# A ring of fourteen gathered pairs in place of ten, in the memory of the split buffers

## The chip, the core and the metric

The kernel runs on one core of a Trainium2 chip. The metric is the device time of one execution in microseconds (us). The engines of the core are named as in the profile: PE is TensorE (matmuls; PEld its weight loads), DVE is VectorE, ACT is ScalarE, POOL is GpSimd and SP is SyncE. All DMAs run on 16 DMA engines that the core has.

## What is computed

Two blocks of two layers each on 256 tokens of width 1024, in float32. The first block holds attention, a convolution and, twice, the `peer_ffn` with which this change deals: each token chooses experts by two small score tables per head, fetches one row of 1024 values from each of two tables for every chosen expert, takes the inner product of the first with its own input, and adds the second rows with the resulting weights.

```python
def peer_ffn(h, w_query, sub_keys, u_tab, v_tab):        # for a block of 128 tokens, 8 heads
    q = (hb @ w_query).reshape(128, PEER_HEADS, 2, half)
    s = jnp.einsum("thpd,hpnd->thpn", q, sub_keys)
    s_top, i_top = lax.top_k(s, PEER_TOPK)               # 16 of 128, in each half
    ...
    best, pos = lax.top_k(cand, PEER_TOPK)               # 16 of the 256 sums
    expert = jnp.take_along_axis(cand_idx, pos, axis=-1)
    gate = jax.nn.softmax(best, axis=-1)
    u = jnp.take(u_tab, expert, axis=0)
    act = jax.nn.gelu(jnp.einsum("thkd,td->thk", u, hb), approximate=False)
    return jnp.einsum("thk,thkd->td", gate * act, jnp.take(v_tab, expert, axis=0))
```

The second block is, per layer, a gated feed-forward (`ffn`), a mixer (`mix`) and another gated feed-forward.

## The kernel before

The phases run in one order on all engines (line 115): ada, attn 0, peer 0, conv 0, peer 1, then ffn, mix, ffn for each of the two layers of the second block. Every engine has its own instruction stream, in order; semaphores tie them together.

**A peer phase.** There are `PICKS` = 256 picks in a layer: 8 heads x 2 token blocks x 16 choices. A pick is one gathered pair for 128 tokens: for each partition (token) one row of 2048 float32, the u row and the v row side by side, 8 KB a partition and 1.05 MB in all. The steps of a pick k:

- GpSimd (lines 805 to 819) issues the indirect gather into slot k % `PAIR_RING` of the ring. Every 16 picks it first waits for the choice that names the experts (`expert_ready`); from pick `PAIR_RING` on it waits until TensorE has used the pair that lay in the slot (`v_used`, line 812). In layer 0 slot 7 is preceded by a wait for TensorE's reads of the attention output that lies there (`LATE_SLOT`).
- VectorE waits for the landing and takes the dot of u with the input (line 2350), and one pick later multiplies by the gate (`weigh`, line 2357).
- ScalarE applies gelu (line 1124) and writes a 128 x 128 diagonal of the weights (line 1131) into one of `DIAGS` = 8 places; from the ninth on it waits for `v_used` too.
- TensorE multiplies diagonal by v into PSUM (line 1727; one call per half of the row, in all four matmul records a pick) and raises `v_used`.
- The last `LAST` = 4 picks of a layer are added up by VectorE (`add_row`, lines 2359 to 2366), which raises `v_used` by 4 at line 2398.

In between, at the picks of `CHOOSE_AT` (line 64), VectorE makes the next choice of 16 experts (`choose`), and at those of `QUERY_AT` TensorE computes the next head's query and scores (lines 1420, 1717), which ScalarE copies out of PSUM (line 997). The phase opens with the first head for token block 0, then the late outputs and norms of token block 1, then the first head for block 1.

GpSimd's other work around the phase: after peer 0 it waits for all of its picks (line 781) and loads 14 weight rows (line 783). SP streams weight tiles of 512 KB into 4 slots (line 727) throughout.

**The memory.** The ring `uv` of ten pairs is the last part of the `arena`, a buffer that every phase carves in its own way. Outside the arena stand `w_hi`, `w_lo`, `a_hi` and `a_lo` (lines 392 to 395), 8 KB a partition each. They hold the two-part splits of weights and activations for the ffn and mix blocks; nothing before the first ffn touches them. The first to write there is ScalarE's `open_split` (called at line 1199, converting at line 896), which in its stream stands right behind the last peer phase's copies of y (line 1158); VectorE subtracts at line 2086.

Line 2968 reserves 4096 bytes a partition for the descriptors of GpSimd's DMAs.

Of the kernel before, what the change touches and what calls it, by code (L numbers as in the profile page):

```python
# [10 lines left out]
F32 = mybir.dt.float32  # L11
# [3 lines left out]
ALU = mybir.AluOpType  # L15
# [4 lines left out]
P = 128  # L20
D = 1024
KC = D // P
# [17 lines left out]
LAYERS = 2  # L40
# [6 lines left out]
HALF = D // 2  # L47
# [7 lines left out]
PICKS = H * TB * TOPK  # L55
SPAN, LAST = 1, 4
# [10 lines left out]
LATE_SLOT = 7  # L67
TAPPED = [6, 7]
EARLY_TAPS = 16
PAIR_RING = 10  # L70
TAP_ROWS = 8
DIAGS = 8
ADA_PARTS = [(0, 0, 4), (0, 4, 12), (1, 0, 4), (1, 4, 12)]
# [298 lines left out]
def bass_two_blocks(nc, stream, mod_rows_in, c_rows, x_cols, ctx_cols, cols_in, const_in, tab_attn, tab_mix, rpb_windows, keys_in, gain_rows,  # L372
# [5 lines left out]
    with ExitStack() as ctx:  # L378
        def sb(name, shape, dt=F32):
            return ctx.enter_context(nc.sbuf_tensor(name, shape, dt))  # L380
# [8 lines left out]
        sq = sb("sq", [P, KC * T])  # L389
        a_in = sq[:, :].rearrange("p (c t) -> p c t", c=KC)  # L390

        w_hi = sb("w_hi", [P, 2, D], F32R)
        w_lo = sb("w_lo", [P, 2, D], F32R)
        a_hi = sb("a_hi", [P, KC, T], F32R)
# [34 lines left out]
        def carve(sizes):  # L429
            at, got = 0, {}  # L430
            for name, n in sizes:
# [32 lines left out]
                  for name in ("ctx", "pt") for e in range(2)]  # L464
# [2 lines left out]
                   ("s2", TB * 2 * NKEY), ("tv", 64), ("ti", 64), ("tf", 64), ("cand", TB * 256), ("cand2", TB * 256),  # L467
                   ("bv", 32), ("bp", 32), ("ab", 128), ("eq", TB * 256), ("res", 64), ("inv", 1), ("idx", PICKS),
                   ("gate", PICKS), ("raw", PICKS), ("act", PICKS), ("w", PICKS), ("diag", DIAGS * P),
                   ("uv", PAIR_RING * 2 * D)])  # L470
        sub_keys = R["keys"].rearrange("p (m n) -> p m n", m=2 * H)
        h_rows = R["hb"].rearrange("p (b n) -> p b n", b=TB)
        pq = R["q"].rearrange("p (r e t) -> p r e t", r=LEAD, e=2)
# [13 lines left out]
        expert = R["idx"].bitcast(U32)  # L487
        gate, act_raw, act_out, act_w = R["gate"], R["raw"], R["act"], R["w"]
        diag = R["diag"].rearrange("p (r n) -> p r n", r=DIAGS)
        pair_ring = R["uv"].rearrange("p (r n) -> p r n", r=PAIR_RING)  # L490
        u_part, v_part = pair_ring[:, :, 0:D], pair_ring[:, :, D:2 * D]
        y_rows = sq[:, :].rearrange("p (b n) -> p b n", b=2 * TB)

        act_ring = sq[:, 0:2 * T].rearrange("p (b t) -> p b t", b=2)
# [276 lines left out]
        def _(pool):  # L771
# [34 lines left out]
            def peer(l):  # L806
                base = PICKS * l
                for k in range(PICKS):
                    if k % TOPK == 0:
                        pool.wait_ge(expert_ready, CHOICES * l + k // TOPK + 1)  # L810
                    if base + k >= PAIR_RING:
                        pool.wait_ge(v_used, base + k - PAIR_RING + 1)
                    if l == 0 and k == LATE_SLOT:
                        last = PL["peer", l]["t_late"][KC - 1]
                        pool.wait_ge(tile_done[last.unit], last.first)
                    pool.indirect_dma_start(  # L816
                        out=pair_ring[:, k % PAIR_RING, :], out_offset=None, in_=experts[l],
                        in_offset=bass.IndirectOffsetOnAxis(ap=expert[:, k:k + 1], axis=0)) \
                        .then_inc(pair_landed[k % PAIR_RING], 16)

# [10 lines left out]
        def _(act):  # L831
# [362 lines left out]
            def ffn(f):  # L1194
                pl = PL["ffn", f]
                l, j = f // 2, f % 2
                s = BLOCKS.index(("ffn", f))
                if s == 0:
                    open_split(f)
                if PART_BASE["ffn", f]:  # L1200
                    act.wait_ge(part_used, PART_BASE["ffn", f])
# [197 lines left out]
        def _(pe):  # L1399
# [301 lines left out]
            def peer(l):  # L1701
# [19 lines left out]
                def values(n):  # L1721
                    b = n % PER_HEAD // PER_CHOICE
                    for k in range(SPAN * n, SPAN * (n + 1)):
                        pe.wait_ge(diag_ready, TURNED * l + k + 1)
                        pe.wait_ge(pair_landed[k % PAIR_RING], landed(l, k))
                        for half in range(2):
                            ins = pe.matmul(ps[:, 2 * b + half, :], diag[:, k % DIAGS, :],  # L1727
                                            v_part[:, k % PAIR_RING, HALF * half:HALF * (half + 1)],
                                            start=(k == TOPK * b), stop=(k == (TURNED if b == TB - 1 else PICKS - TOPK * (TB - 1 - b)) - 1),
                                            skip_group_check=True)  # L1730
                        ins.then_inc(v_used, 1)
# [276 lines left out]
        def _(dve):  # L2008
# [256 lines left out]
            def peer(l):  # L2265
# [79 lines left out]
                def dots(n, first, end):  # L2345
                    b = n % PER_HEAD // PER_CHOICE
                    for k in range(first, end):
                        u = u_part[:, k % PAIR_RING, :]
                        dve.wait_ge(pair_landed[k % PAIR_RING], landed(l, k))
                        dve.scalar_tensor_tensor(out=u, in0=u, scalar=1.0, in1=h_rows[:, b, :], op0=ALU.mult,  # L2350
                                                 op1=ALU.mult, accum_out=act_raw[:, k:k + 1]).then_inc(dot_done, 1)
# [5 lines left out]
                    dve.tensor_tensor(act_w[:, part], act_out[:, part], gate[:, part], ALU.mult).then_inc(weighed, 1)  # L2357

                def add_row(k):
                    row, w = v_part[:, k % PAIR_RING, :], act_w[:, k:k + 1]  # L2360
                    dve.wait_ge(weighed, WEIGHED * l + GROUPS + k - TURNED + 1)
                    if k == TURNED:
                        link(dve.tensor_scalar(row, row, w, None, ALU.mult))
                    else:
                        link(dve.scalar_tensor_tensor(out=row, in0=row, scalar=w, in1=v_part[:, (k - 1) % PAIR_RING, :],
                                                      op0=ALU.mult, op1=ALU.add))

                choose(0)
# [23 lines left out]
                dve.wait_ge(v_used, base + TURNED)  # L2392
                for half in range(2):
                    dve.tensor_tensor(y_rows[:, 2 + half, :], ps[:, 2 + half, :],
                                      v_part[:, (PICKS - 1) % PAIR_RING, HALF * half:HALF * (half + 1)], ALU.add) \
                        .then_inc(y_copied, 1)
                dve.wait_ge(y_copied, 2 * TB * (l + 1))
                dve.sem_inc(v_used, LAST)
# [579 lines left out]
```

## Time and profile before

| | us |
|---|---|
| median of 3 runs | 3013.23 |
| lowest, highest | 3011.79, 3018.31 |
| profiled execution | 3023.53 |
| its span | 3021.7 |
| mean granted TensorE clock in it | 0.947 |
| PE busy | 2624.4 (87%) |
| DVE busy | 1952.7 (65%) |
| ACT busy | 1112.2 (37%) |
| POOL busy | 627.7 (21%) |

The profile is of one execution. Its slices cut the span in 40 equal parts of some 75.5 us; a digit is a tenth of the slice. Windows are stretches in us from the start of the span; their DMA share is the mean busy share of the 16 DMA engines. In the list of groups the idle time behind the last bar is that of the engine just before these instructions, with what ended it. Peer 0 runs from about 338 to 1035 us of the span, peer 1 from about 1200 to 1900 us.

### The profile page before, as it was taken

The page shows a single profiled execution, that of the slowest core. Times are in us where ns is not written, and L with a number is a line of the kernel's source. Part 1 is how long each engine was busy: PE and PEld are TensorE (multiplying, and loading weights), DVE is VectorE, ACT ScalarE, POOL GpSimd, SP SyncE. Part 2 cuts the span into 40 slices and gives each one's busy share as a digit, 9 for nine tenths or more (in the row PEclk, how much of TensorE's full clock was granted, in tenths as well). Part 3 has the DMA queues.
Part 4 walks back from the last instruction along what each step waited for, and adds up shares of the span by engine and source line. Part 5 has one row for each costly group of instructions (what it writes and reads, how often), then busy time and mean ns, then how long its engine had stood idle before and what let it go on. Part 6 is the DMA issues. An engine that isn't in the chain of part 4 may idle for free. (4 is left out here: it accounts for less than half of the span.)

```text
span 3021.7 us, 36197 instructions
## 1 busy us (share of the span) xinstructions
PE 2624.4 (87%) x11546; PEld 1729.6 (57%) x11546; DVE 1952.7 (65%) x4771; ACT 1112.2 (37%) x2639; POOL 627.7 (21%) x600
## 2 busy tenths in 40 slices
PE   7989888888877697788888877799989999999998
PEld 3534744333332386543333332798848989985798
DVE  1866467776676586667766775666746666675565
ACT  3245232222222322322222221445535454464544
POOL 0400134444444200244344443000000000000000
PEclk9989999999989898899999899899989999999999
DMA  9930889999999834899999999455415545552454
GB/s 307 387 150 1 321 327 420 417 413 417 409 415 417 353 110 141 334 409 417 416 419 416 408 413 420 170 187 175 159 53 177 185 160 188 184 161 83 147 183 151
DMA packets 152951, 832.42 MB, mean 275 GB/s; under 512 B 17008, under 2 KB 17136, under 8 KB 86384
## 3 DMA queue, kind: packets, MB, share of 16 engines
q0 software_dynamic: 85392, 579.38, 47.0%
q1 hardware_dynamic: 65664, 238.65, 23.8%
q10 hardware_dynamic: 1760, 12.70, 1.3%
q8 instruction: 71, 1.16, 0.2%
q14 instruction: 64, 0.52, 0.0%
HBM read 829.61 MB, written 1.05 MB: 275 GB/s over the span
## 5 line engine op out<-in xcount | busy, mean ns | idle before, releaser
L1727 PE MATMUL ps<-arena 128*128 128x512 f32 x2016 | 964.1, 626 | 253.7 <-ACT arena L1131 253.4
L1727 PEld LDWEIGHTS ps<-arena 128*128 128x128 f32 x2016 | 382.4, 198 | 825.4 <-ACT arena L1131 431.4
L2350 DVE SCALAR_TENSOR_TENSOR arena<-arena 128x1024 f32<-128x1024 f32 x512 | 626.1, 1224 | 329.5 <-DMA arena<-experts,arena 329.3
L816 POOL DMA_INDIRECT arena<-experts,arena x512 | 571.3, 1116 | 1104.1 <-PE ps L1727 745.9
L2086 DVE TENSOR_TENSOR w_lo<-weights,w_hi 128x512 fp32r<-128x512 f32 x528 | 364.3, 691 | 281.9 <-ACT w_hi L896 280.0
L1131 ACT ACTIVATE arena<-con,arena 128x128 f32<-128x128 f32 x504 | 203.0, 403 | 750.0 <-DVE arena L2357 750.0
L896 ACT ACTIVATE w_hi<-weights 128x512 fp32r<-128x512 f32 x528 | 332.9, 632 | 376.8 <-PE ps L1666 280.1
L1664 PE MATMUL ps<-a_hi,w_hi 128*128 128x256 f32 x1408 | 400.4, 284 | 5.8 <-DVEq L2105 2.7
L1665 PE MATMUL ps<-a_lo,w_hi 128*128 128x256 f32 x1408 | 399.6, 284 | 0.0
L1666 PE MATMUL ps<-a_hi,w_lo 128*128 128x256 f32 x1408 | 399.5, 284 | 0.0
L1664 PEld LDWEIGHTS ps<-a_hi,w_hi 128*128 128x128 f32 x1408 | 271.1, 193 | 10.6 <-DVEq L2105 3.1
L1665 PEld LDWEIGHTS ps<-a_lo,w_hi 128*128 128x128 f32 x1408 | 271.2, 193 | 3.1
L1666 PEld LDWEIGHTS ps<-a_hi,w_lo 128*128 128x128 f32 x1408 | 271.1, 193 | 0.0
L1420 PE MATMUL ps<-sq,weights 128*128 128x256 f32 (+1 forms) x1088 | 210.1, 356 | 22.0 <-ACT sq L890 16.4
L1420 PEld LDWEIGHTS ps<-sq,weights 128*128 128x128 f32 x1088 | 187.1, 202 | 48.6 <-issue 24.4
L997 ACT ACTIVATE arena<-ps 128x256 f32<-128x256 f32 (+5 forms) x182 | 83.3, 462 | 236.3 <-PE ps L1420 136.1
L1675 PE MATMUL ps<-w_hi,v_hi 128*128 128x512 f32 x352 | 138.5, 394 | 4.7 <-DVE v_lo L2506 4.7
L1675 PE MATMUL ps<-w_hi,v_lo 128*128 128x512 f32 x352 | 138.1, 392 | 0.0
L1675 PE MATMUL ps<-w_lo,v_hi 128*128 128x512 f32 x352 | 137.0, 389 | 0.0
L2357 DVE TENSOR_TENSOR arena<-arena 128x1 f32<-128x1 f32 x512 | 79.9, 156 | 73.1 <-ACT arena L1124 73.0
L2060 DVE SCALAR_TENSOR_TENSOR arena<-arena,mod_rows 128x1024 f32<-128x1024 f32 x71 | 93.6, 1344 | 33.5 <-DMA arena<-mod_rows_in 32.3
L1420 PE MATMUL ps<-arena,weights 128*128 128x128 f32 (+3 forms) x480 | 104.9, 378 | 4.4 <-ACT arena L890 2.2
(274 smaller groups left out, 3090.4 us busy)
## 6 DMA issues: line engine op xcount, KB each, us to landing
weights<-stream SPq DMA_DIRECT2D x453, 512.0 KB
arena<-mod_rows_in POOLq DMA_DIRECT2D x71, 512.0 KB, 8.8
arena<-experts,arena POOLq DMA_INDIRECT x512
mod_rows<-mod_rows_in POOLq DMA_DIRECT2D x9, 512.0 KB, 8.7
arena<-gain_rows ACTq DMA_DIRECT2D x1, 3072.0 KB, 11.5
arena<-rpb_windows ACTq DMA_DIRECT2D x4, 512.0 KB, 17.5
arena<-keys_in ACTq DMA_DIRECT2D x2, 1024.0 KB, 7.6
arena<-tab_mix ACTq DMA_DIRECT2D x2, 768.0 KB, 4.1
```

Source lines behind the costliest of these rows:

```text
L816: pool.indirect_dma_start(out=pair_ring[:, k % PAIR_RING, :], out_offset=None, in_=experts[l], in_offset=bass.IndirectOffsetOnAxis(ap=expe ...
L896: act.activation(w_hi[:, o % 2, part], weights[:, t.unit, part], ACT.Copy).then_inc(hi_ready, 1)
L1131: act.activation(diag[:, k % DIAGS, :], const("ident"), ACT.Copy, scale=act_w[:, k:k + 1]).then_inc(diag_ready, 1)
L1420: ins = pe.matmul(dst, wt(t, k, a, b), rhs(k), start=(k == 0), stop=(k == KC - 1))
L1664: pe.matmul(dst, w_hi[:, o % 2, cut], a_hi[:, k, :], start=(k == 0), stop=False)
L1665: pe.matmul(dst, w_hi[:, o % 2, cut], a_lo[:, k, :], start=False, stop=False)
L1666: ins = pe.matmul(dst, w_lo[:, o % 2, cut], a_hi[:, k, :], start=False, stop=(k == KC - 1))
L1675: ins = pe.matmul(ps[:, 2 * tb + half, :], v[:, b, at], w[:, o % 2, cut], start=(start and n == 0), stop=False, skip_group_check=True)
L1727: ins = pe.matmul(ps[:, 2 * b + half, :], diag[:, k % DIAGS, :], v_part[:, k % PAIR_RING, HALF * half:HALF * (half + 1)], start=(k == TOPK ...
L2060: dve.scalar_tensor_tensor(out=tile, in0=tile, scalar=1.0, in1=c_row, op0=ALU.mult, op1=ALU.mult, accum_out=mod[:, l, m, 0:1]).then_inc(ro ...
L2086: dve.tensor_tensor(w_lo[:, o % 2, part], weights[:, t.unit, part], w_hi[:, o % 2, part].bitcast(F32), ALU.subtract) \
L2350: dve.scalar_tensor_tensor(out=u, in0=u, scalar=1.0, in1=h_rows[:, b, :], op0=ALU.mult, op1=ALU.mult, accum_out=act_raw[:, k:k + 1]).then_ ...
```

## The change

The ring gets fourteen slots. Slots 0 to 9 stay in the arena. Slots 10 to 13 lie in a tensor `held` of 32 KB a partition that is laid out at the place of `w_hi`, `w_lo`, `a_hi` and `a_lo`, which are then laid out over it: one pair a buffer. `pair_of`, `u_of` and `v_of` give a pick's slot in either place. There are fourteen landing semaphores in place of ten. ScalarE waits, ahead of the first split of the first ffn, until `v_used` is 2 x 256 - 4 = 508, which is when TensorE has used its last pair. The number of gathers, dots, diagonals and matmuls is as before.

```diff
-PAIR_RING = 10
+ARENA_PAIRS = 10
+PAIR_RING = ARENA_PAIRS + 4
@@
+        with nc.sbuf_tensor("held", [P, KC, D], F32) as held:
+            pass
         w_hi = sb("w_hi", [P, 2, D], F32R)
         w_lo = sb("w_lo", [P, 2, D], F32R)
         a_hi = sb("a_hi", [P, KC, T], F32R)
@@
-                   ("uv", PAIR_RING * 2 * D)])
+                   ("uv", ARENA_PAIRS * 2 * D)])
@@
-        pair_ring = R["uv"].rearrange("p (r n) -> p r n", r=PAIR_RING)
-        u_part, v_part = pair_ring[:, :, 0:D], pair_ring[:, :, D:2 * D]
+        arena_pairs = R["uv"].rearrange("p (r n) -> p r n", r=ARENA_PAIRS)
+        held_pairs = held[:, :, :].rearrange("p r n -> p (r n)").rearrange("p (r n) -> p r n", r=PAIR_RING - ARENA_PAIRS)
+
+        def pair_of(k):
+
+            r = k % PAIR_RING
+            return arena_pairs[:, r, :] if r < ARENA_PAIRS else held_pairs[:, r - ARENA_PAIRS, :]
+
+        def u_of(k):
+            return pair_of(k)[:, 0:D]
+
+        def v_of(k, a=0, b=D):
+            return pair_of(k)[:, D + a:D + b]
@@
-                        out=pair_ring[:, k % PAIR_RING, :], out_offset=None, in_=experts[l],
+                        out=pair_of(k), out_offset=None, in_=experts[l],
@@
                 if s == 0:
+                    act.wait_ge(v_used, PICKS * LAYERS - LAST)
                     open_split(f)
@@
-                                            v_part[:, k % PAIR_RING, HALF * half:HALF * (half + 1)],
+                                            v_of(k, HALF * half, HALF * (half + 1)),
@@
-                        u = u_part[:, k % PAIR_RING, :]
+                        u = u_of(k)
```

The other uses of `u_part` and `v_part` are replaced in the same way.

## Rows read from the trace of the kernel before

**Rows 1.** The page's 40 slices: DMA engines' busy tenths, and GB/s moved.
```profile
DMA  9930889999999834899999999455415545552454
GB/s 307 387 150 1 321 327 420 417 413 417 409 415 417 353 110 141 334 409 417 416 419 416 408 413 420 170 187 175 159 53 177 185 160 188 184 161 83 147 183 151
```

**Rows 2.** Groups of instructions: busy us, mean ns | idle us before, its releasers.
```profile
L2350 DVE SCALAR_TENSOR_TENSOR arena<-arena 128x1024 f32<-128x1024 f32 x512 | 626.1, 1224 | 329.5 <-DMA arena<-experts,arena 329.3
L816 POOL DMA_INDIRECT arena<-experts,arena x512 | 571.3, 1116 | 1104.1 <-PE ps L1727 745.9 <-DVE arena L2334 324.2 <-issue 33.7
...
L1420 PE MATMUL ps<-arena,weights 128*128 128x128 f32 (+3 forms) x480 | 104.9, 378 | 4.4 <-ACT arena L890 2.2 <-DMA weights<-stream 1.7 <-ACT arena L997 0.5
```

**Rows 3.** Busy time by window; the last columns are PEclk, DMA share, GB/s.
```profile
337.00:445.00 108.00, 86.49 (x327) 55.66 (x326) 66.40 (x218) 34.01 (x97) 34.02 (x32) 0.91 0.88 350
445.00:1025.00 580.00, 466.38 (x1072) 200.83 (x1071) 397.99 (x1161) 155.16 (x514) 251.37 (x224) 0.94 1.01 416
1200.00:1310.00 110.00, 89.55 (x332) 57.75 (x331) 69.86 (x227) 34.34 (x97) 36.47 (x34) 0.89 0.88 349
1310.00:1885.00 575.00, 461.91 (x1064) 198.96 (x1062) 395.64 (x1156) 149.50 (x494) 249.45 (x223) 0.93 1.01 416
```

**Rows 4.** The start of peer 0 in windows: POOL busy, PEclk, DMA share, GB/s.
```profile
345.00:355.00 10.00, 3.79 (x5) 0.65 1.02 420
...
375.00:385.00 10.00, 2.29 (x2) 1.00 0.76 286
...
395.00:405.00 10.00, 2.84 (x3) 1.00 0.65 231
405.00:415.00 10.00, 2.69 (x2) 0.66 0.42 150
...
435.00:445.00 10.00, 6.47 (x6) 1.00 0.94 360
```

**Rows 5.** POOL in order of time: start, duration, [idle before <-releaser].
```profile
349.07 0.95 POOL L816 DMA_INDIRECT arena<-experts,arena  x1 [0.30 <-issue]
367.57 0.94 POOL L816 DMA_INDIRECT arena<-experts,arena  x1 [17.56 <-PE ps L1727]
...
1004.58 0.94 POOL L816 DMA_INDIRECT arena<-experts,arena  x1 [1.55 <-PE ps L1727]
...
1230.76 0.95 POOL L816 DMA_INDIRECT arena<-experts,arena  x1 [17.64 <-PE ps L1727]
```

**Rows 6.** Who waited for whom, 335 to 445 us: us in total, times, longest.
```profile
POOL arena L816 <- PE ps L1727: 67.7, 17, 17.6
```

**Rows 7.** The same, VectorE's dots: first line 2350 over 335 to 1030 us, then 445 to 1030 us.
```profile
  DMA arena<-experts,arena: 164.2, 141
...
DVE arena L2350 <- DMA arena<-experts,arena: 164.2, 141, 2.2
```

**Rows 8.** VectorE in order of time, 440 to 470 us.
```profile
445.39 1.23 DVE L2350 SCALAR_TENSOR_TENSOR arena<-arena 128x1024 f32<-128x1024 f32 x1 [0.96 <-DMA arena<-experts,arena]
...
456.88 0.16 DVE L2341 TENSOR_REDUCE arena<-arena 128x1 f32<-128x16 f32 x1
...
466.70 1.22 DVE L2350 SCALAR_TENSOR_TENSOR arena<-arena 128x1024 f32<-128x1024 f32 x1
```

**Rows 9.** TensorE in order of time, 440 to 560 us, neighbours of a line merged.
```profile
439.57 20.36 PE L1727 MATMUL ps<-arena 128*128 128x512 f32 x47
468.49 28.89 PE L1727 MATMUL ps<-arena 128*128 128x512 f32 x60 [8.56 <-ACT arena L1131]
...
499.58 7.07 PE L1420 MATMUL ps<-sq,weights 128*128 128x256 f32 x32
```

**Rows 10.** The end of peer 1 in order of time, TensorE and ScalarE.
```profile
1888.50 1.99 PE L1727 MATMUL ps<-arena 128*128 128x512 f32 x4 [0.50 <-ACT arena L1131]
...
1898.18 1.15 ACT L896 ACTIVATE w_hi<-weights 128x512 fp32r<-128x512 f32 x2
```

**Rows 11.** POOL's fourteen plain loads of 512 KB behind peer 0.
```profile
1037.17 7.39 POOL L783 DMA_DIRECT2D arena<-mod_rows_in  x14 [24.17 <-DVEq L2398]
```

More of the change, by code:

```diff
@@ L2359, in add_row @@
                 def add_row(k):
-                    row, w = v_part[:, k % PAIR_RING, :], act_w[:, k:k + 1]
+                    row, w = v_of(k), act_w[:, k:k + 1]
                     dve.wait_ge(weighed, WEIGHED * l + GROUPS + k - TURNED + 1)
@@ L2364, in add_row @@
                     else:
-                        link(dve.scalar_tensor_tensor(out=row, in0=row, scalar=w, in1=v_part[:, (k - 1) % PAIR_RING, :],
+                        link(dve.scalar_tensor_tensor(out=row, in0=row, scalar=w, in1=v_of(k - 1),
                                                       op0=ALU.mult, op1=ALU.add))
@@ L2394, in peer @@
                     dve.tensor_tensor(y_rows[:, 2 + half, :], ps[:, 2 + half, :],
-                                      v_part[:, (PICKS - 1) % PAIR_RING, HALF * half:HALF * (half + 1)], ALU.add) \
+                                      v_of(PICKS - 1, HALF * half, HALF * (half + 1)), ALU.add) \
                         .then_inc(y_copied, 1)
```

## The prediction

> **What bounds the kernel now.** I read the page's slices first. In the two stretches in which a `peer` phase gathers experts (slices 5 to 13 and 17 to 24) the DMA digits stand at 8 and 9 and the rate at 409 to 420 GB/s, while in the later blocks it is 50 to 190 GB/s [rows 1]. So the two gather stretches are limited by bytes, and nothing of the blocks behind them is. The costliest groups agree: VectorE's dot line 2350 sat idle 329.5 us, nearly all of it until a gathered pair landed, and GpSimd's gather line 816 sat 745.9 us until TensorE had used a pair, that is until a slot of the ring came free [rows 2]. Read carelessly, the second number promises hundreds of microseconds. It does not: a full ring costs time only where the DMA engines run dry meanwhile.
>
> That is what the long windows tell. A saturated stretch shows a DMA share of 1.01 (the scale reads a little over one). From 445 to 1025 us and from 1310 to 1885 us the share is 1.01: no idle worth naming in 580 and 575 us. The first 108 and 110 us of the two phases have 0.88 [rows 3]. Idle there is 108 x (1.01 - 0.88) = 14.0 us and 110 x 0.13 = 14.3 us. The ten-microsecond windows of layer 0 place it: four windows at 0.76, 0.65, 0.42 and 0.94 lose 2.5 + 3.6 + 5.9 + 0.7 = 12.7 us; the window with the first gathers queued is full at 1.02 and 420 GB/s [rows 4].
>
> Why it idles there: the tenth gather is issued at 349.07, and the eleventh waits 17.56 us, to 367.57, for the first pair to be used; layer 1 repeats it, 17.64 us, to 1230.76 [rows 5]. In the opening 110 us GpSimd waits 67.7 us for TensorE in 17 waits [rows 6]. In the same time the dots never wait for a landing: their waits of the whole phase, 164.2 us in 141, all fall after 445 us [rows 7], and the first is at 445.39 [rows 8]. So up to 445 us the pairs are used at a pace set by the chain of scores, choices, queries and diagonals; from then to the end of the phase the pace is the DMA's.
>
> **The change part by part.** *Four more pairs.* While the chain sets the pace, slots come free at the same times as before, but gathers 11 to 14 go out at about 350 to 355 us, right behind the tenth, and each later one four uses earlier. The DMA engines then work through the idle of [rows 4] until the ring of fourteen is full too; all they can gain is four pairs, since whenever they are dry, ten landed pairs stand unused before and fourteen after. When the chain catches up, it finds four more pairs landed than before, and the rest of the phase, which goes at the DMA's pace, ends earlier by what four pairs take. One pair takes 0.94 + 1.55 = 2.49 us in steady state (the spacing of gathers) [rows 5], so 4 x 2.49 = 9.96 us per phase. It fits in the idle that is there: 12.7 us in layer 0, and by the same share some 13 us in layer 1. Two phases: 19.9 us. The ends are 0 (the lead is not taken or not kept) and 12.7 us a phase (all idle after the first fill goes).
>
> A page of the Trainium skill (DMA: Bandwidth & Descriptors, Specifications) puts the HBM limit of one core at about 358 GB/s; a pair of 1.05 MB would then take 2.93 us and the four of both layers 23.4 us. The rows show 420 GB/s on this core, so the measured spacing is used.
>
> *Does the lead survive to the end?* It has to be used up by the chain without the DMA engines running dry again. Between two choices lie 16 picks. TensorE needs 20.36 / 47 x 4 = 1.73 us for a pick's four matmuls [rows 9], 27.7 us for 16, and every other time a query of 7.07 us plus its keys, some 4.2 us on average; the DMA needs 16 x 2.49 + 1.2 for a weight tile (512 KB at 420 GB/s) = 41.0 us. VectorE needs 9.8 us for a choice (456.88 to 466.70) [rows 8] and 16 x 1.22 = 19.5 us for dots. Both engines have some 9 to 11 us of slack per 16 picks, if TensorE's stall of 8.56 us at a choice [rows 9] shrinks. It does: with pairs already landed VectorE dots at 1.22 us a pick against TensorE's 1.73, reaches the choice earlier, and TensorE still has diagonals in hand (up to eight) while it chooses. So the lead is turned into time within one or two choices, by some 500 us. Even if not, the last picks of a phase have no choices, (line 64 places the last at pick 208), and there the chain gains 2.49 - 1.73 = 0.76 us a pick, over 44 picks.
>
> *The small dips behind 445 us.* The share of 1.01 leaves at most 1 to 2 us in each phase; I take 1 us for both together, ends 0 and 3.
>
> *The ACT wait.* `open_split` of the first ffn now waits for `v_used` 508, all of TensorE's uses of pairs. TensorE's last value matmuls end at 1888.50 + 1.99 = 1890.5; ScalarE reaches the split at 1898.18 [rows 10], behind two copies of y. Cover 7.7 us, cost nothing. Queued behind it are the rest of the first split and the row norms, for which VectorE (line 2086) and TensorE wait; the cover goes only if TensorE ends 7.7 us later against ScalarE's tail, and the four last rows, which VectorE adds, tie the two together. The last four picks (252 to 255) fall in slots 0 to 3, in the arena, so nothing that VectorE still reads is under `w_hi`.
>
> *Slots and semaphores.* The same instructions with other addresses and constants, one wait more: 0. Layer 1's first gather asks for fewer uses than before, but stands behind the wait for all of layer 0's on GpSimd (line 781): 0. The wait before slot 7 in layer 0 is the same. The weight tiles share the DMA engines with a longer gather queue; with ten queued TensorE waited for tiles 1.7 us in all at the line that uses them in these phases [rows 2]. I take 0, ends 0 and 2 us.
>
> *Sum.* -19.9 - 1 = -20.9 us. The profiled execution took 3023.5 us (span 3021.7 and 1.8 around it) and would take 3002.6. The median of the runs is 10.3 us below that execution, 3013.2; the gain is in stretches bound by bytes and waits, so it is taken from it whole: **2992.3 us**.
>
> **Rivals.** *Part of the lead is given back.* If TensorE's stall does not shrink, 27.7 + 4.2 + 8.56 = 40.5 us stand against the DMA's 41.0: the chain keeps standing four pairs behind, with as many in flight as now, and any disturbance dries the DMA engines. Half the lead lost gives 3013.2 - 10 = 3003. For it speaks that TensorE is busy 466.38 of the 580 us [rows 3]; against it the dots' idle of 164.2 us and the picks without choices. *The queue does not take fourteen.* Then GpSimd stalls in the issue in place of the wait, and the time stays 3013. Against it: fourteen plain loads were queued in one go in 7.39 us [rows 11]. The Trainium skill (DMA: Bandwidth & Descriptors, Terms and The descriptor swizzle) gives 16 bytes a descriptor and nine descriptors per engine and direction for a transfer of 1 MiB; by that the 4096 bytes a partition that line 2968 reserves would hold 28 gathers, as an estimate that no row here shows. *All idle goes.* If the better fed chain also runs quicker at the start, 2 x 12.7 + 2 = 27 us: 2986. *The longer queue lowers the rate.* With thirteen gathers in flight in place of nine, HBM or the weight tiles between them might cost rate over the 1155 saturated microseconds. It turns the sign where 1155 us x loss exceeds 20.9 us, at 1.8%, that is where the 416 GB/s of these stretches fall below 408; at 2.5% the time is 3013.2 - 20.9 + 28.9 = 3021. Against it: right after the first burst, with the most ever in flight, the window reads 420 GB/s, no less than the 416 of the long stretches with their tiles [rows 3, 4].
>
> **How the numbers follow.** Chances: the forecast 0.74 (its own range 2988 to 2997, from the tiles and dips and the spread of the runs), lead half lost 0.10, queue too short 0.05, all idle gone 0.07, lower rate 0.04. The range reaches from the third rival to the first, 2984 to 3004, and leaves out about one in ten. 0.2% is 6 us, about what a measurement of this kernel can tell from no change. Faster by more than that is below 3007.2: 0.74 + 0.07 and most of the first rival, 0.89; within it the queue case and the rest, 0.07; slower 0.04.
>
> **What would show it.** Fourteen gathers issued 1.25 us apart at the start of both phases, the fifteenth at some 367 us; the windows from 375 us near 1.01 up to some 405; the dots' first wait for a landing near the same time or a little later but four picks further on; the value matmuls of layer 1 ending at about 1870 in place of 1890.5; layer 1's start 10 us earlier, the first ffn 20 us earlier, everything behind it unchanged in length; no wait of ScalarE before the first split. I am wrong if the pairs' spacing rises above 2.49 us, if the DMA share dips below 1 after 450 us, or if the chain's first 100 us change length.

## The result and the profile after

The kernel with fourteen slots takes **2986.65 us** (median of 4 runs, 2983.76 to 2989.93) against 3014.14 us (4 runs, 3011.79 to 3018.31) for the kernel before in the same set. The ratio is 0.9915 with a 95% interval of 0.9902 to 0.9929, that is 21 to 30 us and in the middle 25.6 us; the two medians themselves are 27.5 us apart. The forecast was 2992.3 us, a gain of 20.9 us: the sign and the range held, the gain was larger than the sum. Of the executions below, one of the ten of before_again took 3746.48 us, is a slow one, and is left out of its ratio.

The first view is the page of the kernel after: the 40 slices with the DMA engines' busy tenths and the rate, as in [rows 1].

```profile
DMA  9940899999999734999999998555425555542454
GB/s 299 391 163 1 300 419 420 420 420 420 421 420 420 304 99 140 420 417 420 420 420 420 420 420 355 183 183 168 156 67 183 183 161 184 183 161 75 150 188 148
```

Slices 5 to 12 now stand at 419 to 421 GB/s, where before they began at 327 and then ran between 409 and 420; in the second phase the slices at 409 and 408 are gone. The busy time by window answers [rows 3]; the last three columns are the granted clock, the DMA share and GB/s.

```profile
337.00:445.00 108.00, 92.44 (x347) 58.09 (x346) 75.50 (x253) 37.77 (x108) 46.55 (x42) 0.95 1.01 413
445.00:1003.00 558.00, 450.22 (x1045) 193.27 (x1044) 386.10 (x1122) 150.13 (x498) 241.18 (x215) 0.94 1.01 420
1185.00:1295.00 110.00, 94.12 (x360) 59.60 (x359) 77.68 (x249) 36.79 (x107) 45.62 (x40) 0.94 1.01 409
1295.00:1855.00 560.00, 453.76 (x1053) 195.99 (x1051) 389.62 (x1140) 147.07 (x485) 243.59 (x217) 0.95 1.01 420
1850.00:1860.00 10.00, 8.05 (x17) 2.71 (x16) 5.34 (x15) 2.02 (x9) 0.00 (x0) 1.00 0.57 234
```

The opening of both phases is full: a share of 1.01 where [rows 3] had 0.88. GpSimd in order of time (start, duration, idle before and its releaser) answers [rows 5]: the eleventh gather goes out behind the tenth, four of the first fourteen go to the new slots, and the fifteenth comes at 359.60 us.

```profile
349.06 1.09 POOL L830 DMA_INDIRECT arena<-experts,arena  x1 [0.31 <-issue]
350.46 1.94 POOL L830 DMA_INDIRECT held<-experts,arena  x1 [0.30 <-issue]
...
355.21 0.94 POOL L830 DMA_INDIRECT held<-experts,arena  x1 [0.30 <-issue]
359.60 0.95 POOL L830 DMA_INDIRECT arena<-experts,arena  x1 [3.45 <-PE ps L1742]
```

The dots' waits for landings, VectorE in order of time, answer [rows 8]. Apart from one wait of 0.5 us at the second dot, the first is here, before the 42nd dot; in the kernel before it was at 445.39, before the 29th.

```profile
462.64 1.23 DVE L2365 SCALAR_TENSOR_TENSOR held<-held,arena 128x1024 f32<-128x1024 f32 x1 [0.62 <-DMA held<-experts,arena]
```

In layer 1 it is the 44th dot, 130.2 us after the first gather, where it had been the 29th at 108.5 us. The end of layer 1's phase, TensorE and ScalarE in order of time, answers [rows 10].

```profile
1858.01 1.98 PE L1742 MATMUL ps<-held,arena 128*128 128x512 f32 x4 [0.47 <-ACT arena L1145]
...
1867.66 1.15 ACT L910 ACTIVATE w_hi<-weights 128x512 fp32r<-128x512 f32 x2
```

The last value matmul ends at 1859.99 in place of 1890.5, 30.5 us earlier, and the cover of the new wait before the split is 7.7 us as before. Measured from the first gather to the last value matmul, the two phases took 689.0 and 689.65 us before and 671.26 and 672.17 us after. That is 17.7 and 17.5 us where I had forecast 10 each. The spans differ by 33.6 us, more than the medians do, since the profiled execution before lay 10.3 us above its median. Beside the phases' 35.2 us, the stretch between them (from the last value matmul of layer 0 to the first gather of layer 1) is 4.9 us longer after, 178.97 against 174.09, and the one behind the last value matmul 3.1 us shorter, 1128.15 against 1131.25.

**Something else had changed between the two profiles.** In the kernel before the first dot starts 17.1 us after the first gather (337.74 to 354.85); in the kernel after it starts after 10.5 us (337.58 to 348.12), although nothing of the change touches what lies between. These are ScalarE and VectorE of the kernel before:

```profile
346.27 1.71 ACT L993 ACTIVATE sq<-h_res 128x128 f32<-128x128 f32 x8 [11.89 <-remote]
352.00 0.37 ACT L878 ACTIVATE rstd<-ps,con 128x128 f32<-128x128 f32 x1 [4.02 <-remote]
...
354.85 1.22 DVE L2350 SCALAR_TENSOR_TENSOR arena<-arena 128x1024 f32<-128x1024 f32 x1
```

and the same steps in the kernel after:

```profile
342.76 1.71 ACT L1007 ACTIVATE sq<-h_res 128x128 f32<-128x128 f32 x8 [8.53 <-PE ps L1435]
345.27 0.37 ACT L892 ACTIVATE rstd<-ps,con 128x128 f32<-128x128 f32 x1 [0.81 <-PE ps L1450]
...
348.12 1.22 DVE L2365 SCALAR_TENSOR_TENSOR arena<-arena 128x1024 f32<-128x1024 f32 x1
```

ScalarE squares the late residual once TensorE has finished an output of line 1420 (1435 after). In the kernel before that matmul ended at 342.88 and its semaphore rose at 346.25, 3.4 us later; the sum of squares ended at 349.37 and its semaphore rose at 351.98, 2.6 us later. In the kernel after both rose within 0.02 us of the end. I call these **late reports**. Behind them everything up to the first dot waits. TensorE's reports are not all that is concerned: in every profile with late reports the sum's matmul itself ended 1.2 to 2.5 us after ScalarE's last square, in the others 0.5 to 0.8 us, so a report of ScalarE may have been late too. I had read the 14 us of idle in [rows 3, 4] as one thing, the chain with ten slots; part of it was this.

### The profile page after: what moved, and what is told of

Its sections match the earlier page's. It is cut to its first block and busy times, and to the rows that moved or that the text cites. A ratio compares the mean times of both kernels' runs of the same rounds, so it can differ in the third digit from the quotient of the medians.

```text
span 2988.1 us, 36198 instructions
## 1 busy us (share of the span) xinstructions
PE 2612.3 (87%) x11546; PEld 1723.9 (58%) x11546; DVE 1952.1 (65%) x4771; ACT 1112.4 (37%) x2639; POOL 633.9 (21%) x600
## 5 line engine op out<-in xcount | busy, mean ns | idle before, releaser
L1742 PE MATMUL ps<-arena 128*128 128x512 f32 x1440 | 683.3, 619 | 162.4 <-ACT arena L1145 162.2
L2365 DVE SCALAR_TENSOR_TENSOR arena<-arena 128x1024 f32<-128x1024 f32 x368 | 450.1, 1224 | 227.4 <-DMA arena<-experts,arena 227.3
L1742 PEld LDWEIGHTS ps<-arena 128*128 128x128 f32 x1440 | 268.3, 195 | 562.8 <-ACT arena L1145 292.1
L830 POOL DMA_INDIRECT arena<-experts,arena x368 | 413.1, 1123 | 847.4 <-PE ps L1742 487.4
L1742 PE MATMUL ps<-held,arena 128*128 128x512 f32 x576 | 277.8, 625 | 79.6 <-ACT arena L1145 79.6
L1742 PEld LDWEIGHTS ps<-held,arena 128*128 128x128 f32 x576 | 109.8, 199 | 244.6 <-ACT arena L1145 131.9
L2365 DVE SCALAR_TENSOR_TENSOR held<-held,arena 128x1024 f32<-128x1024 f32 x144 | 175.9, 1222 | 83.5 <-DMA held<-experts,arena 83.5
L830 POOL DMA_INDIRECT held<-experts,arena x144 | 163.8, 1138 | 199.1 <-PE ps L1742 184.4
```

The lines of the kernel that those rows point to most:

```text
L830: pool.indirect_dma_start(out=pair_of(k), out_offset=None, in_=experts[l], in_offset=bass.IndirectOffsetOnAxis(ap=expert[:, k:k + 1], axis ...
```

## The experiments

Ratios are to the kernel before, run beside them on the same chip; a phase is measured from its first gather to its last value matmul. The four sets of experiments ran on four different chips. The kernel before had a median of 3014.1 us in the set of the result, and of 3012.3, 3023.7, 3008.3 and 3023.5 us in these four, which will matter. None of the kernels leaves out or changes a part of the computation.

**First set: how deep, and when.** Fourteen slots keep their places; only GpSimd's wait is bound to a depth, so that the code and the memory are those of after and fewer gathers are in flight:

```diff
-                    if base + k >= PAIR_RING:
-                        pool.wait_ge(v_used, base + k - PAIR_RING + 1)
+                    depth = 10
+                    if base + k >= depth:
+                        pool.wait_ge(v_used, base + k - depth + 1)
```

with `depth` 10, 12, `10 if k < 64 else 14` (late_only) and `14 if k < 64 else 10` (start_only).

> The changed kernel with its fourteen slots, their places and the wait of ScalarE, but GpSimd keeps at most ten pairs out: the same computation. Depth theory (all of the gain is how many pairs may be out): the time of the kernel before, ratio 1.000 within 0.002. Placement theory (addresses, semaphores or the place of the instructions give some of it): faster than before, down to 0.997, which would be the 7 us by which the change beat the forecast.

Measured: 3008.71 us, ratio 0.9986 (0.9976 to 0.9996), within what the depth theory expects. So the depth carries nearly all of the gain: with it taken away 3.6 us are left.

> Fourteen slots, at most twelve pairs out. Lead theory (each pair more is gained once per phase, 2.49 us): 2 x 2 x 2.49 = 10 us, ratio 0.9967. Lead and rate theory (the saturated stretch too goes faster with a deeper queue, 416 to 420 GB/s, 5.5 us a phase at fourteen): 10 us and some 5 to 11 more, 0.993 to 0.995.

Measured: 2991.35 us, ratio 0.9932 (0.9914 to 0.995); the phases take 673.9 and 677.0 us. The ratio is not that of the lead theory (0.9967) and lies at the border of the lead and rate theory. The phases speak for the lead alone: they are 5.9 and 4.6 us shorter than those of depth10, where two pairs are 4.98 us. The medians are 17.4 us apart, and the 7 us that the phases do not explain stay open; late_only below shows that they are not the higher rate behind the opening.

> At most ten pairs out for the first 64 picks of a phase, fourteen from then on. Lead theory as in the forecast: the lead is made in the opening, so 1 us or nothing is left, ratio 0.9995 or above. Rate theory: the dips of the saturated stretch (windows of 392 to 398 GB/s in the kernel before) go, 5 us a phase, 0.9965, and the windows behind 450 us read 420 GB/s in place of 416.

Measured: 3007.77 us, ratio 0.9988 (0.9976 to 0.9999); phases 680.9 and 681.3 us. The window from 448 to 1000 us has 420 GB/s, as the rate theory says, but the time is that of depth10: the rate theory's 0.9965 is refuted.

> Fourteen pairs out for the first 64 picks of a phase, ten from then on. Lead theory: 20 us of gain stay, ratio 0.9934. Rate theory: the same 20 us, and the 7 us above them are lost; the windows behind 550 us are back at 416 GB/s. If the lead is not turned into time by pick 64, part of it is lost as well, and the ratio lies between 0.994 and 1.

Measured: 2989.48 us, ratio 0.9922 (0.9897 to 0.9947); phases 674.0 and 674.2 us. The gain of the full depth stays.

The windows of the opening, here of layer 0 in depth10, late_only and start_only, show what the depth does there:

```profile
338.00:448.00 110.00, 94.44 (x349) 57.79 (x348) 71.17 (x227) 35.48 (x103) 42.98 (x39) 0.95 0.95 382
```

```profile
338.00:448.00 110.00, 94.45 (x338) 58.02 (x337) 70.32 (x225) 35.49 (x103) 41.92 (x38) 0.92 0.94 378
```

```profile
338.00:448.00 110.00, 94.45 (x339) 58.15 (x339) 75.19 (x251) 37.78 (x108) 46.17 (x42) 0.92 1.00 411
```

A depth of ten at the opening gives 0.95 and 0.94, fourteen gives 1.00 (and twelve, in depth12, 0.99), and only kernels that have more than ten there are quicker. A late depth without an early one brings nothing. None of the four kernels shows a late report, and as in the kernel after their first dot comes 10.5 us after the first gather in layer 0 and 11.6 us in layer 1.

So the clean comparison of depths is depth10 with after, neither of which has late reports: 679.84 and 681.59 us against 671.26 and 672.17, which is **8.6 and 9.4 us a phase** for four slots, against 9.96 forecast. The rest of the difference between the two profiles, 689.0 to 679.8 and 689.65 to 681.6, is 9.2 and 8.1 us, of which the later first dot is 6.6 and 5.6. Both figures rest on one profile of either kernel; a second one of the kernel after without late reports, after_third below, has 671.7 and 672.9 us.

Where along the phase is it gained? The dots, in us from the first gather of layer 0, depth10 and after: the 16th at 67.1 and 66.9, the 32nd at 108.6 and 101.4, the 64th at 191.4 and 182.7, the last at 683.9 and 675.3. The lead is made between the 16th and the 64th dot and carried to the end unchanged: from the 64th to the last dot they take 492.4 and 492.6 us. That is odd beside the rate, 416 GB/s in depth10 and 420 after, which over 558 us would be 5.3 us. Here are the long window of depth10 and its last 10 us of transfers in layer 1:

```profile
448.00:1018.00 570.00, 457.34 (x1051) 196.78 (x1049) 394.01 (x1153) 153.66 (x508) 244.23 (x218) 0.93 1.01 416
1870.00:1880.00 10.00, 6.83 (x15) 2.09 (x13) 5.98 (x14) 1.68 (x7) 0.00 (x0) 1.00 0.94 390
```

In depth10 the DMA engines stand at 0.94 in the last 10 us before the dots' last waits; in the kernel after the corresponding window (1850 to 1860, above) is at 0.57, while VectorE still waits for landings at a pair's usual pace:

```profile
1856.21 1.23 DVE L2365 SCALAR_TENSOR_TENSOR arena<-arena 128x1024 f32<-128x1024 f32 x1 [1.15 <-DMA arena<-experts,arena]
...
1858.69 1.23 DVE L2365 SCALAR_TENSOR_TENSOR arena<-arena 128x1024 f32<-128x1024 f32 x1 [1.18 <-DMA arena<-experts,arena]
```

So the mean rate rose without the pairs becoming complete any sooner, and the bytes that were ahead came back as idle engines at the end. The reason is that some of the sixteen engines run ahead of the slowest. Each gather has sixteen landing reports, one from each engine, and the traces hold the time of every one. Here is the mean time from the first to the last report of a gather in layer 0, in us, by picks:

```
kernel       64 to 127   128 to 191   192 to 239
depth10         2.6          2.6          2.6
start_only      2.9          2.7          2.4
after           4.4          7.0          9.1
late_only       3.1          5.8          8.0
```

With fourteen out behind pick 64 the leading engines draw away from the slowest all along the phase; with ten out they do not, and the dips must be their idle time, which is inferred. A pair is complete with its last report. The mean report of the last pair comes 7.1 us before its last one in the kernel after and 2.2 us in depth10, and at the 64th pair these are 1.8 and 1.1 us: of the 5.3 us of transfers that the higher rate is worth, 4.2 us are bytes of engines that were ahead. The Trainium skill (DMA: Bandwidth & Descriptors, Why a DMA increments its semaphore by 16 and not by 1) says that the engines finish independently and that only the full sixteen means that all data has landed; the trace agrees. Which engines lag, and why, is open.

**Second set: the layout, and a repeat.** `ten_held` has a ring of ten of which four lie in the new memory (`PAIR_RING = 10`, six slots in the arena), with the new wait of ScalarE; `depth13` is as above; the kernels before and after ran once more under other names.

> The kernel before, unchanged, for a second profile. In the profile of before the first dot of a phase comes 17.1 us after the first gather, in every kernel with fourteen slots 10.5 to 11.6 us. Code theory (something in the old kernel's layout holds TensorE there): 17 us in both phases again, and a time 4 us above that of ten pairs out in the new layout. Chance theory (a stall of that one execution): 10.5 to 11.6 us, and the ratio of this run to before is 1.000.

Measured: 3025.48 us, ratio 0.9999 (0.9986 to 1.0011). The first dots come 17.2 us after the first gather in both layers, as the code theory says; after_again and the fourth set bear on that theory.

> A ring of ten, six pairs in the arena and four in the memory of the split buffers, with the wait of ScalarE: the same computation. Depth theory: the time of the kernel before within 0.2%. Placement theory: the memory of the held pairs gives the 0.14% that ten pairs out gained in the layout of fourteen, ratio 0.9986, and this kernel's phases open like those.

Measured: 3017.97 us, ratio 0.9984 (0.9973 to 0.9995). The memory and the wait cost nothing. The ratio is the placement theory's 0.9986, but the phases do not open like those of depth10 (first dots at 17.2 us) and are no shorter than in before_again (689.2 and 687.4 us against 688.0 and 689.0), so the theory's reason is not shown.

> Fourteen slots, at most thirteen pairs out. Lead theory: one pair less than the change in each phase, 5 us longer, some 2991 us. Saturation theory (with twelve out the DMA engines are nearly dry-free: 2991 us and a share of 0.99 in the opening): the last two pairs bring little, 2987 to 2990 us.

Measured: 3009.8 us, ratio 0.9951 (0.9934 to 0.9968), some 19 us above what both theories expect; phases 683.3 and 684.5 us. The reason shows in the next run, beside which thirteen pairs are no slower than fourteen.

> The changed kernel again, beside the others on one chip: 0.9915 within 0.0015, phases of 671 to 672 us from the first gather to the last value matmul, opening stretch at a DMA share of 1.01. If it is within 0.001 of the thirteen pairs, the opening is saturated before the fourteenth.

Measured: 3012.76 us, **ratio 0.996** (0.9946 to 0.9974). The expectation of 0.9915 was missed: the same kernel that had gained 25.6 us gained 11 to 12 us here, and its interval does not meet the first one. Its ScalarE and VectorE at the start of layer 0's phase:

```profile
350.15 1.71 ACT L1007 ACTIVATE sq<-h_res 128x128 f32<-128x128 f32 x8 [11.90 <-remote]
361.45 0.37 ACT L892 ACTIVATE rstd<-ps,con 128x128 f32<-128x128 f32 x1 [9.59 <-remote]
```

```profile
362.19 2.19 DVE L2172 SCALAR_TENSOR_TENSOR sq<-h_res,gain,rstd 128x128 f32<-128x128 f32 x8 [10.91 <-ACT rstd L896]
364.30 1.22 DVE L2365 SCALAR_TENSOR_TENSOR arena<-arena 128x1024 f32<-128x1024 f32 x1
```

The late reports are there, in the code that had shown none, and the second is far later. All four kernels of this set have them. Here is the second report (the sum of squares) in every profile with late reports, in us, for layer 0 / layer 1; the last column is the report's time less the end of the burst's last gather:

```
kernel, gathers in the burst   matmul ends   report rises   after the burst's end
before, 10                     349.37 / 1213.62   351.98 / 1215.16   1.96 / 2.05
before_again, 10               351.34 / 1213.28   353.05 / 1214.82   1.98 / 2.01
before_third, 10               352.30 / 1215.36   354.36 / 1216.88   1.92 / 1.98
ten_held, 10                   352.65 / 1217.70   354.15 / 1217.86   2.01 / 2.05
depth13, 13                    349.59 / 1206.34   356.06 / 1212.03   2.44 / 2.48
after_again, 14                354.22 / 1212.78   361.43 / 1219.86   2.55 / 2.60
```

Whenever the matmul ends, before the burst's end or after, its report comes 1.9 to 2.6 us after GpSimd's last gather of the burst. So where reports are late this one waits for the burst, and each further slot, at 1.25 us of issue, makes it later: the first dot comes 17.2 us after the first gather with ten, 21.4 with thirteen, 22.7 with fourteen. Fourteen slots give two things at once there: four pairs of lead, 8.6 and 9.4 us, and a chain that starts 5.5 and 5.6 us later in the two layers. The phases went from 687.96 and 689.01 to 684.35 and 683.48 us, 3.6 and 5.5 us, and the median by 10.9.

**The same six profiles lack records.** They hold 24481 to 24540 updates of semaphores, the eight without late reports 24758 or 24759. DMA landings are missing (8079 to 8118 of the gathers' 8192) and, in the first 20 us of layer 0's phase, updates of VectorE and ScalarE too: 79 to 135 updates of all engines are recorded there against 200 to 216. Whether these updates were merged on their way or only not written down the traces don't tell, so it is not excluded that the recording has a part in the late reports.

**Third set: is it the burst?** The kernel after with a pause in the burst, until VectorE has normalized the first chunk of the late columns:

```diff
                     if base + k >= PAIR_RING:
                         pool.wait_ge(v_used, base + k - PAIR_RING + 1)
+                    if k == 4:
+                        pool.wait_ge(scaled_ready, FEEDS[f"late{l}"] - KC + 1)
```

This is burst4; burst7 has `k == 7`.

> The kernel after once more, as the partner of the two below. On record so far: 0.9915 of before in its first set of runs and 0.9960 in its second, where the profile showed the sum of squares of the late outputs (TensorE L1450) ended 12.6 us after the first gather but its semaphore update only at 19.8 us, 2.55 us after the fourteenth gather; with ten slots in the same runs the update came 2.0 us after the tenth, at 14.3 us. Theory H (held updates): the profile falls in one of two patterns. Held: first dot 22.7 us after the first gather, phases near 684 us, ratio near 0.996. Free: first dot at 10.5 us, phases near 671 us, ratio near 0.9915. Nothing between. Rival C (the second set only had a generally slower chip): every stretch is longer by the same share, and the first dot takes any value.

Measured: 2986.87 us (5 runs), ratio 0.9924 (0.9901 to 0.9948). The phases are 671.7 and 672.9 us, the first dot of layer 0 comes at 10.54 us, and there is no late report: theory H's free pattern.

> The kernel after, but GpSimd issues only four gathers of each phase at first and waits for the first chunk of the late norm (DVE L2172) before the other ten. Theory H in the held pattern: four gathers end 4.8 us after the first began, before the first update that was held (its matmul ends at 5.1 us), so neither update is late; the sum's update comes at 7.7 us, the ten gathers start near 8.8 us, four queued pairs (4 x 2.49 = 10.0 us) cover that. First dot near 10.5 us instead of 22.7, so 12 us less per phase, some 24 us in all: ratio to before near 0.988 to 0.989 if before is held too. Rival M (the hold moves along): any burst of gathers holds what TensorE reports meanwhile, so the late outputs' sums (L1435, ending near 15 us) are held until 2 us after the second burst, near 23 us, the first value matmul comes near 30 us and the gain is under 5 us per phase. Rival P (a fixed property of the spot, whatever GpSimd does): the first update is still 3.4 us late. In the free pattern: the same as after_third within 2 us.

Measured: 2984.7 us, ratio 0.9915 (0.9887 to 0.9942). GpSimd's row for the fifth gather shows the pause:

```profile
349.95 1.08 POOL L832 DMA_INDIRECT arena<-experts,arena  x1 [4.36 <-DVE sq L2174]
```

> The same with seven gathers ahead of the wait. Theory H in the held pattern: the first update still comes 8.5 us after the first gather (3.4 us late, with the end of the seventh gather), the sum then ends at 12.6 us and its update is on time, since the burst ended at 8.5 us; gathers eight to fourteen start near 13.6 us; first dot near 15.6 us instead of 22.7, so 7 us less per phase, 14 us in all: ratio near 0.9915. Rival M: as in burst4, the update of the late outputs' sums is held by the second burst (13.6 to 22.4 us). Rival P: the sum's update stays late by 6 us or more although no gather is being issued. In the free pattern: the wait ends at 8.8 us, when the eighth gather would start anyway: the same as after_third within 2 us.

Measured: 2986.9 us, ratio 0.9926 (0.9897 to 0.9954).

The chip of this set gives no late reports, so the pause could not show its use; it shows only that it is free, as expected (within 2.2 us of after_third): four queued pairs cover 4.4 us of it, and the phase of layer 0 is 671.6 and 671.1 us against 671.7, that of layer 1 673.7 and 673.4 against 672.9. Whether a split burst wins back the 11 us where reports are late was not tried on such a chip, and stays open.

**Fourth set: code or place?**

> The kernel before itself, a third profile. Both so far show the two TensorE updates held during the burst of ten gathers (first dot 17.1 us after the first gather, phases 688 to 689.7 us, span near 3021 us), while its medians of 3008 to 3014 us in two sets of runs are 10 to 15 us below the 3024 us of the set in which every profile showed them held. Theory H (held or free is a matter of where the program runs, not of its code): in a set whose before median is near 3010 us the profile is free: first dot near 10.5 us, phases near 680 and 681.5 us as with fourteen slots held at a depth of ten, DMA share of the first 110 us near 0.95 instead of 0.88, conv phase some 5 us longer, span 3007 to 3011 us. In a set whose median is near 3024 us it is held as before. Rival K (the held updates belong to the code of the kernel before, and fourteen slots free them): first dot at 17.1 us and phases near 689 us whatever the set's median. Ratio 1.000 in both.

Measured: 3022.89 us (10 runs), ratio 1.0004 (0.9989 to 1.0018), beside a median of 3023.53 us for the same kernel. The profile has both late reports, first dots at 17.07 and 17.11 us and phases of 688.73 and 688.71 us: what theory H expects of a set near 3024 us. By itself it doesn't refute the rival that the kernel before always has them, since all three of its profiles do. Two other things speak against that rival. The kernel after shows both forms with the same code, at 3012.8 and at 2986.7 us. And in the first set the kernel before (3012.3 us) was only 3.6 us behind depth10, which has no late reports; with them it should be some 12 us behind, by the 6.6 and 5.6 us of the first dots. In the second and fourth set, where its profiles have them, its medians are 11 us higher (3023.7 and 3023.5), though on other chips. A profile of the kernel before without late reports was never caught, so that half rests on its times.

## Why the prediction was right, and where it was not

**What bounds it.** Right: both phases are bound by bytes except at the opening, and the kernel with a depth of fourteen only there takes nearly all of the gain. The reading of [rows 1] was too smooth: of the slices named, counted from 0, slice 5 has 327 GB/s, slice 13 353 and slice 22 408, not 409 to 420.

**Four more pairs, 9.96 us a phase.** Right to about a tenth: 8.6 and 9.4 us, depth10 against after. What is missing may be room: at a depth of ten and without late reports the opening already moves 382 GB/s (share 0.95, where [rows 3] have 350 and 0.88), and the kernel after 413, so in 110 us it gets 31 x 110 = 3.4 MB or 3.3 pairs ahead, not four, which is 8.1 us. But the lead grows on behind these windows: over the first 192 us of the phase the rates are 396 and 416 GB/s, 3.7 pairs, and in layer 1 over 193 us 394 and 416, 4.0 pairs. So where the last tenth stays is open. The idle of 12.7 to 14.3 us in [rows 3, 4], into which I had fitted four pairs, was partly the late reports'. The page of the Trainium skill that I had set beside it (DMA: Bandwidth & Descriptors, Specifications, 358 GB/s) would have made it 11.7 us a phase, an estimate; the measured lead is below even what 2.49 us a pair gives.

**The lead survives.** Right: the dots of after are 8.7 us ahead at the 64th and 8.6 us ahead at the last. The step by which the lead becomes time was right too, TensorE's stall at a choice. At the first choice behind the opening it shrinks from 8.56 us [rows 9], and 9.05 us in layer 1, to 2.19 us in both layers:

```profile
453.05 1.99 PE L1742 MATMUL ps<-arena 128*128 128x512 f32 x4 [2.19 <-ACT arena L1145]
```

It does so once: at the seven choices after that it is 9.05 us again, as before the change. By then the lead is used up, and the dots wait for landings.

**The small dips, 1 us.** The dips did go: with the depth back at ten behind pick 64 the window from 448 to 1000 us has 415 GB/s, with fourteen 420. Their worth is within the scatter of single profiles in spite of 1%. From the 64th dot to the last, start_only (ten out there) needs 493.7 and 493.3 us and after 492.6 and 492.5, but depth10, with ten throughout, needs 492.4 and 492.7, and late_only, with fourteen there, 492.6 and 491.3. Nothing here shows my 1 us, which had ends of 0 and 3.

**The ACT wait, slots, semaphores, tiles: 0.** Right: 7.7 us of cover at the end of layer 1, ten_held no slower than before, no fall in rate.

**The sum.** The forecast of 20.9 us stands against 25.6 us in the set of the result and 21 to 23 us in the third set (3008.3 - 2986.9 = 21.4; by the ratio 22.9). Of these, the depth explains 8.6 + 9.4 = 18.0 us by phases. The rest, 3 to 8 us, is not tied to a mechanism: depth10 keeps 0.14% and ten_held 0.16% ahead of the kernel before at the same depth, and I found no stretch to put it in. Single profiles do not resolve it. The stretch between the two phases took 178.5 to 179.0 us in four profiles (depth10, after, after_third, burst4) and 172.4 to 174.5 us in the other ten, and the one behind the last value matmul 1124.1 to 1131.8 us, neither by depth: before_again took 1131.8 us there and before_third, the same kernel, 1126.3.

**The rivals.** *All idle goes* named 2986 us, and the median came there; its reason, that the chain runs quicker at the start, is what the profile after shows, but fourteen slots are not its cause. On the chips with late reports the change even makes the chain start later. So the time agrees with that rival largely by coincidence. There was luck in the forecast as well: it was worked out from a profile with late reports and tested where the profile has none. Where they are present the gain was 10.9 us, by the medians, half of the 20.9. *Part of the lead is given back*, 3003 us, had a stall of TensorE that does not shrink and disturbance in the middle of the phase in mind; the stall shrank where it had to, and the real give-back sits at the opening, 11 us of 20, and only on some chips. *The queue does not take fourteen* and *the longer queue lowers the rate* are refuted by fourteen gathers 1.25 us apart, or nearly, and by 420 GB/s.

**What I said would show it.** The gathers' spacing and the windows at 1.01 are there. But the dots' waits for landings began at 462.64 us, 17 us later and thirteen picks further on, not about the same time and four; the fifteenth gather came at 359.60, not 367, the value matmuls of layer 1 ended at 1860, not 1870, and the chain's first 100 us did change length, which I had named as a sign of being wrong. It was the right sign to name: it exposed that my profile of before was probably not the baseline of the runs beside it. The warning stood in my own working: a profiled execution 10.3 us above the median. I took the gain from it whole, with the reason that its parts are bound by bytes and waits; the waits labelled "remote" at the start of each phase were in view and not asked about.

## What to carry to other kernels

A ring costs time only where its consumer is slower than the transfers for a while; count the pairs that the producer can be ahead when the consumer catches up, and check that this stretch is idle for the reason you think. A higher mean rate in a long saturated stretch is not yet a gain: look at when the pieces become complete, that is at the last of their sixteen landing reports. A long burst of indirect gathers can hold back reports that another engine needs at that moment, so where a latency chain runs beside it, try a pause after a few gathers: it cost nothing here, and its gain was not shown. And when a profiled execution stands well off the median of its own kernel, look for a wait in it that other executions may lack before using it as the baseline; run the unchanged kernel on a second chip.

## What the runs showed of the hardware

- TensorE's semaphore reports can come up to 7.2 us after the matmul's end while GpSimd issues indirect gathers of 1 MiB, at 1.25 us each. It happened in both layers of six profiles, the first of before and the five of the second and fourth set, and in none of the eight others, whatever the code. Where it happened, the report of the matmul that ends 5.1 us after the first gather rose 8.5 to 8.6 us after it, with the end of the seventh gather (9.9 us in layer 1 of ten_held), and the report of the sum of squares 1.9 to 2.6 us after the last gather of the burst. Why the chips differ, through what the report waits, and what the missing records have to do with it, is open.
- In the profiles with late reports the gathers of a burst start evenly, 1.25 to 1.31 us apart. In the others single ones among the first fourteen take up to 2.15 us in place of 0.94. The median time from issue to landing in the kernel after was 26 us.
- With fourteen gathers out, the sixteen landing reports of one gather came 4.4 us apart at picks 64 to 127 and 9.1 us at picks 192 to 239 of layer 0; with ten out 2.6 us throughout.
- One core took 420 GB/s from HBM for 560 us on end. The Trainium skill (Perfetto Trace Analysis, Roofline) says that a lone core can exceed the 358 GB/s share and is bounded at about 435 GB/s by its sixteen DMA engines; the trace agrees.
